# A mixture-of-experts layer: expert rows added by indirect DMA to a sum in DRAM instead of stored and fetched back

## The reference

```
s = sigmoid(x1 @ router_w); two experts per token, from the best of 4 groups
gate = s of the two, divided by their sum
out = sum over the two: gate * ((silu(x1 @ w_gate[e]) * (x1 @ w_up[e])) @ w_down[e])
result = LayerNorm(alpha * x1 + out) * ln2_w + ln2_b
```

## Time and profile before

| | us |
|---|---|
| median of the three runs | 1034.89 |
| span of the profiled execution | 1030.7 |
| TensorE busy in it | 884.6 (86%) |
| VectorE / ScalarE / POOL busy | 667.7 / 455.7 / 139.0 |
| first expert tile starts | 514.1 |
| last matmul ends | 948.8 |

### The profile page before, as it was taken

The page is one execution under the profiler, slowest core; times in us unless marked ns, Lnnn a source line. Parts: engine busy times, 40 slices in busy tenths (PEclk is TensorE's granted clock), DMA queues, the critical chain, the costliest instruction groups (busy, mean ns, idle before and its releaser), DMA issues.

```text
span 1030.7 us, 15075 instructions
## 1 busy us (share of the span) xinstructions
PE 884.6 (86%) x4992; PEld 772.3 (75%) x4992; DVE 667.7 (65%) x981; ACT 455.7 (44%) x594; POOL 139.0 (13%) x168
## 2 busy tenths in 40 slices
PE   6999999999967999995199999999999999998000
PEld 6998887888755888884189898988989898897000
DVE  3441899983265778874837586676898662635695
ACT  3531110102355443313336686767888662645231
POOL 3000011011112112100100001000110100000583
PEclk9999999999996999996599999999999999999555
DMA  7620213314225433314657498695999863595671
GB/s 270 214 83 1 99 54 123 105 73 160 82 85 164 157 108 100 125 41 160 229 224 284 167 405 345 219 392 181 413 407 410 339 224 142 185 324 205 212 259 79
DMA packets 77509, 202.25 MB, mean 196 GB/s; under 512 B 7215, under 2 KB 27009, under 8 KB 77473
## 3 DMA queue, kind: packets, MB, share of 16 engines
q1 hardware_dynamic: 63984, 155.31, 41.8%
q0 software_dynamic: 9888, 33.76, 9.1%
q10 hardware_dynamic: 3600, 12.72, 3.1%
HBM read 167.14 MB, written 34.62 MB: 196 GB/s over the span
## 4 chain that ended last, share of the span: by engine, by line
PE 79%; DVE 9%; issue 7%; DMA 2%; ACT 1%; POOL 1%; DVEq 0%; SPq 0%; POOLq 0%; ACTq 0%
PE banks L1072 17%; PE banks L622 13%; PE banks L611 13%; PE banks L636 13%; PE banks L1069 8%; PE banks L1186 6%; PE banks L595 2%; DVE arena L849 2%; PE banks L1207 2%; PE banks L602 1%; PE banks L1053 1%; DMA arena<-in_x 1%; DVE split_weights L804 1%; PE banks L1121 1%; DVE small L865 1%
## 5 line engine op out<-in xcount | busy, mean ns | idle before, releaser
L804 DVE TENSOR_TENSOR split_weights<-arena,split_weights 128x1024 fp32r<-128x1024 f32 x192 | 223.7, 1218 | 1.0
L654 ACT ACTIVATE split_weights<-arena 128x1024 fp32r<-128x1024 f32 x192 | 190.7, 1052 | 12.2 <-ACT work L691 10.4
L1072 PE MATMUL banks<-split_weights 128*128 128x512 f32 (+2 forms) x960 | 182.5, 351 | 0.0
L1072 PEld LDWEIGHTS banks<-split_weights 128*128 128x128 f32 x960 | 156.2, 191 | 23.9 <-issue 1.4
L622 PE MATMUL banks<-split_weights,split_rows 128*128 128x256 f32 x1152 | 147.5, 284 | 0.0
L622 PEld LDWEIGHTS banks<-split_weights,split_rows 128*128 128x128 f32 x1152 | 142.7, 191 | 1.9
L611 PE MATMUL banks<-split_weights,split_rows 128*128 128x512 f32 x576 | 136.0, 392 | 2.5 <-DVE split_rows L808 2.5
L636 PE MATMUL banks<-split_weights,split_hidden 128*128 128x512 f32 x576 | 137.5, 394 | 0.0
L611 PEld LDWEIGHTS banks<-split_weights,split_rows 128*128 128x128 f32 x576 | 109.1, 190 | 25.6 <-issue 2.9
L636 PEld LDWEIGHTS banks<-split_weights,split_hidden 128*128 128x128 f32 x576 | 106.6, 188 | 21.6
L821 DVE TENSOR_TENSOR work<-work,banks 128x256 f32<-128x256 f32 x48 | 20.2, 421 | 116.0 <-PE banks L622 116.0
(11 more groups left out here) (294 smaller groups left out, 991.2 us busy)
## 6 DMA issues: line engine op xcount, KB each, us to landing
arena<-in_w_gate SPq DMA_DIRECT2D x64, 512.0 KB, 6.2
arena<-in_w_up SPq DMA_DIRECT2D x64, 512.0 KB, 7.2
arena<-in_w_down SPq DMA_DIRECT2D x64, 512.0 KB, 7.9
y_scratch<-work ACTq DMA_DIRECT2D x24, 512.0 KB, 6.6
arena<-in_w_in SPq DMA_DIRECT2D x20, 512.0 KB, 5.5
arena<-in_x SPq DMA_DIRECT2D x16, 512.0 KB, 6.1
arena<-in_w_out SPq DMA_DIRECT2D x8, 512.0 KB, 5.1
x_scratch<-arena SPq DMA_DIRECT2D x8, 512.0 KB, 3.4
```

Source lines behind the costliest of these rows:

```text
L654: act.activation(unit_split(u, 0), unit_slot(u), AF.Copy).then_inc(xw_hi, 1)
L804: dve.tensor_tensor(unit_split(u, 1), unit_slot(u), unit_split(u, 0).bitcast(F32), ALU.subtract).then_inc(xw_lo, 1)
L1072: last = pe.matmul(b[:, 0:width], xT[:, hx, k, j * P:(j + 1) * P], wc[:, hw, k, 0:width], start=(k == 0 and i == 0), stop=(k == KC - 1 and ...
```

## The change

- The mixer stage stores each x1 tile twice: in `x1_dram` and in a new `acc_dram`. Both have 128 rows more at their start, filled with ones, for slots that hold no token; token t is row 128 + t.
- Routing also computes the gate of each slot: three bf16 parts of the gates (divided by alpha) on the one-hots, 16 matmuls, and a sum, `gate_slot`. A second list of rows, `tok_sums`, gives each unused slot a row of its own among the 128. All this comes before the first tile's rows are split.
- ScalarE's copy of a tile's result multiplies it by the slot's gate. Its store is gone. POOL instead adds the 128 rows to `acc_dram` by an indirect DMA with `compute_op=ALU.add`, each add after the one before has landed.
- The last stage waits for all adds, loads 8 tiles of `acc_dram` and normalises them on VectorE (LayerNorm doesn't change if its input is divided by alpha and its epsilon by alpha squared). ScalarE only takes the square root. POOL does nothing in it. The rows `ln2` are loaded at the start of the expert stage.

The core of the diff:

```diff
             def store_x1(ch):
                 sp.wait_ge(x1_ready, ch.c + 1)
-                sp.dma_start(x1_dram[bass.ds(ch.c * P, P), :], x1s).then_inc(x1_out, 16)
+                for rows_out in (x1_dram, acc_dram):
+                    sp.dma_start(rows_out[bass.ds(P + ch.c * P, P), :], x1s).then_inc(x1_out, 16)
...
+            def add_rows(g):
+                pool.wait_ge(y_out, ADDED + 16 * g)
+                pool.tensor_copy(tok_out, tok_sums[:, bass.ds(g, 1)]).then_inc(out_idx_ready, 1)
+                pool.wait_ge(y_sb, PRIMED + g + 1)
+                wait_apart(pool, out_idx_ready, g + 1)
+                pool.indirect_dma_start(out=acc_dram, out_offset=bass.IndirectOffsetOnAxis(ap=tok_out, axis=0), in_=ys,
+                                        in_offset=None, compute_op=ALU.add).then_inc(y_out, 16)
+
+            def body(e, g, last, more):
+                gather(g + 1)
+                add_rows(g)
...
             gather(0, True)
-            total = each_tile(pool, "pool", lambda e, g, last, more: gather(g + 1))
+            for i, src in enumerate((ln2_w[0], ln2_b[0])):
+                pool.dma_start(ln2[:, i, :], src.partition_broadcast(P)).then_inc(y_out, 16)
+            pool.wait_ge(sum_index_ready, 1)
+            total = each_tile(pool, "pool", body)
...
-            wait_apart(pool, y_out, PRIMED + total * 16)
...
+            wait_apart(pool, y_out, ADDED + total * 16)
+            pool.sem_inc(acc_done, 1)
...
+            pe.wait_ge(gate_hot_ready, 1)
+            for i in range(2 * T):
+                last = pe.matmul(bank(3)[:, 0:96], hot_lo[:, i, :], hot_gate[:, i, :], start=(i == 0), stop=(i == 2 * T - 1))
+            last.then_inc(gate_sums_ps, 1)
             transpose_rows(0)
...
                 act.wait_ge(y_ps, g + 1)
-                act.wait_ge(y_out, PRIMED + g * 16)
-                act.activation(ys, psum[:, 2:4, :].rearrange("p a n -> p (a n)"), AF.Copy).then_inc(y_sb, 1)
-                act.wait_ge(y_sb, PRIMED + g + 1)
-                act.dma_start(y_dram[bass.ds(g * P, P), :], ys).then_inc(y_out, 16)
+                act.wait_ge(y_out, ADDED + g * 16)
+                act.activation(ys, psum[:, 2:4, :].rearrange("p a n -> p (a n)"), AF.Copy,
+                               scale=gate_slot[:, bass.ds(g, 1)]).then_inc(y_sb, 1)
...
+            dve.wait_ge(tok_ready, 1)
+            own.link(dve.tensor_scalar(unused, tok[:, :], 0.0, i_tok, ALU.is_equal, ALU.mult))
+            dve.tensor_tensor(tok_sums[:, :], tok[:, :], unused, ALU.add).then_inc(sum_index_ready, 1)
...
+            own.link(dve.tensor_copy(gate_parts[:, 0], gflat2))
+            own.link(dve.tensor_tensor(gate_rest, gflat2, gate_parts[:, 0], ALU.subtract))
+            own.link(dve.tensor_copy(gate_parts[:, 1], gate_rest))
+            own.link(dve.tensor_tensor(gate_parts[:, 2], gate_rest, gate_parts[:, 1], ALU.subtract))
+            for i in range(3):
+                last = dve.tensor_tensor(hot_gate[:, :, i * 32:(i + 1) * 32], hot_tile,
+                                         gate_parts[:, i].unsqueeze(2).to_broadcast([P, 2 * T, 32]), ALU.mult)
+            last.then_inc(gate_hot_ready, 1)
...
-            for u in range(6):
+            for u in range(2):
+                split_lo(0, u)
+            dve.wait_ge(gate_sums_ps, 1)
+            own.link(dve.tensor_copy(gate_sum, bank(3)[:, 0:96]))
+            own.link(dve.tensor_tensor(gate_sum[:, 32:64], gate_sum[:, 32:64], gate_sum[:, 64:96], ALU.add))
+            dve.tensor_tensor(gate_slot, gate_sum[:, 0:32], gate_sum[:, 32:64], ALU.add).then_inc(gates_ready, 1)
+            for u in range(2, 6):
                 split_lo(0, u)
...
+            def finish(t):
+                r = rs_f[:, t:t + 1]
+                dve.wait_ge(fin_std, t + 1)
+                own.link(dve.reciprocal(r, r))
+                dve.scalar_tensor_tensor(final(t), final(t), r, ln2[:, 1, :], ALU.mult, ALU.add).then_inc(out_ready, 1)
+
+            dve.wait_ge(y_out, ADDED)
+            for t in range(T):
+                dve.wait_ge(acc_in[t], 16)
+                for i in range(2):
+                    last = dve.bn_stats(st_c[:, i, :], final(t)[:, i * 512:(i + 1) * 512])
+                wait_apart(dve, dve_own, own.done(last))
+                dve.bn_aggr(mv_f[:, t, :], st_c).then_inc(fin_stats, 1)
+                dve.wait_ge(fin_stats, t + 1)
+                own.link(dve.scalar_tensor_tensor(final(t), final(t), mv_f[:, t, 0:1], ln2[:, 0, :], ALU.subtract, ALU.mult))
                 if t > 0:
+                    finish(t - 1)
+            finish(T - 1)
```

More of the change, by code:

```diff
@@ L51 @@
 TILES_MAX = (2 * SEQ + NE * (P - 1)) // P
-SMALL = 1136
+SMALL = 1160
 UNITS = 12
@@ L68 @@
 PRIMED = 1
+ADDED = 32
 class Chunk:
@@ L321, in hybrid_kernel @@
         packed_sum = at("c", 2)[0:1]
+        gate_rest = at("c", 2 * T)
+        gate_sum = at("c", 96)
+        unused = at("c", 32)
+        gate_parts = at("c", 24).bitcast(BF16).rearrange("p (i n) -> p i n", i=3)
+        hot_gate = at("c", 48 * T * 2).bitcast(BF16).rearrange("p (i n) -> p i n", n=96)
+        used["d"] = 3072
         sil = at("d", DE)
@@ L498, in sp_experts, with final @@
                     load_unit(sp, e, u)
[L500 to L511, removed]
             sp.wait_ge(xw_lo, UNITS * NE)
-            for t in range(SETS):
-                reload_x1(t)
+            sp.wait_ge(acc_done, 1)
             for t in range(T):
-                if t == T - 1:
-                    sp.wait_ge(y_fill, sp.snap(filled))
+                sp.dma_start(final(t), acc_dram[P + t * P:P + (t + 1) * P, :]).then_inc(acc_in[t], 16)
+            for t in range(T):
                 sp.wait_ge(out_ready, t + 1)
[L520 to L530, removed]
+                sp.dma_start(out_tiles[t], final(t)).then_inc(stored, 16)
+            sp.wait_ge(stored, 16 * T)
+        def final(t):
+            return arena[:, t * D:(t + 1) * D]
         def pool_experts(pool, own):
@@ L566, in pool_experts @@
-            for t in range(3):
-                fetch(t)
-            pool.wait_ge(ln2_in, 32)
-            for t in range(T):
-                if t + 3 < T:
-                    fetch(t + 3)
-                pool.wait_ge(scaled_ready, t + 1)
-                pool.tensor_tensor(final(t, 0), final(t, 0), ln2[:, 1, :], ALU.add).then_inc(out_ready, 1)
+            wait_apart(pool, y_out, ADDED + total * 16)
+            pool.sem_inc(acc_done, 1)
         def pe_experts(pe):
@@ L897, in _ @@
                 n += 1
+            sp.wait_ge(made, 3)
+            for rows_out in (x1_dram, acc_dram):
+                sp.dma_start(rows_out[0:P, :].rearrange("p (k n) -> p k n", k=KC),
+                             ones[:, :].unsqueeze(1).to_broadcast([P, KC, P])).then_inc(rows_filled, 16)
             def load_kqv(ch):
@@ L960, in _ @@
             own = Links(pool, sem("pool_own"), "pool_links")
-            for s in (lg_read, x1_out, x1T_ps, lg_ps, y_sb, y_out):
+            for s in (lg_read, x1_out, x1T_ps, lg_ps, y_sb):
                 pool.sem_inc(s, PRIMED)
```

83 lines of the change are left out of this document (24 added, 59 removed).

## The result

The changed kernel takes **1125.14 us** (median of 4 runs, 1121.69 to 1127.24) against 1033.54 us before in the same session: a ratio of 1.089, 95% interval [1.086, 1.092]. It is 92 us slower where I forecast 27, and above my range. The profiled execution took 1121.69 us with a span of 1119.9, so 1.8 us lie outside the span, not the 4.2 I took.

The account below looks back on a forecast made before the run. TensorE paces the expert stage (18.04 us tiles), then a tail without matmuls. Span 1030.7 - 24.6 + 3.9 + 47.6 = 1057.6 us; with 4.2 outside it 1061.8, say 1062 us; range 1021 to 1095.

Parts of the forecast that it names:

- The tail: After the last tile's copy: replacing fetches, scaled additions and POOL's bias additions by reloads and VectorE work saves 24.6 us.
- Before the first tile: Added routing operations on VectorE ahead of the first tile's row split cost 3.9 us, bounds 2.5 and 5.8.
- The moved gather: In each tile POOL's gather of rows two tiles ahead follows the copy wait and add: 14 x 3.4 = 47.6 us.
- S+14.8: Predicted landing of the gather with weights arriving, in us after the tile's gate matmuls start (S); 3.4 us late.
- rival B: TensorE's clock falls in the stalls: 14 x 1.6 = 22 us more, 1084 us; chance 0.13.
- its instruction 0.97 us: In each tile, the time assumed for POOL to issue the add, from S+2.55.
- the constant: Time outside the profiled span, taken as 4.2 us: the median of the runs less the span.
- ScalarE loses the issue of the store: In each tile ScalarE no longer issues the store and gains a scale in its copy; counted as nearly free.
- the 14 tiles with weights arriving: The expert-stage tiles expected to stall, 3.4 us each; the 9 without arriving weights would lose next to nothing.
- Stalls also in the tiles without weights: Expert-stage sign that the forecast was wrong, pointing to rival C or a longer POOL loop than assumed.
- rival C: The add is slow everywhere: gather 11.5 us late in 23 tiles, 265 us more, about 1280 us; chance 0.07.
- the rule I did cite: A DMA that adds issues two reads per piece and halves the rate; used for the add's extra 2.4 us pass.

Follow-up runs that it names:

- The last experiment: The kernel with the gather ahead of the add, plus a final 128x1 POOL copy after VectorE's last result: 1011.5 us, against 1007.24 without it.

## Why the prediction was wrong

**The tail** was 24.6 us by my count and is 31.6: from the copy's end to the end of the span 80.7 before and 49.1 after. From the copy's end to the reloads it takes 1078.20 - 1070.83 = 7.4 us (counted 7.7 + 0.9), to VectorE's start 3.4 more (3.5), then VectorE 35.3 (36.0). The larger part of the 7 us is the end of the program: I carried over 8.0 us, and it is 3.05. The last experiment shows that POOL being last is worth 4 to 5 us.

**Before the first tile**: the first gate matmul starts at 516.70, after a routing chain that began 1.3 us earlier than before. 516.70 - 514.13 + 1.3 = 3.87 us for 3.9.

**The moved gather and the clock behind it** are where the prediction failed, in two steps. The mechanism of the first stands: the wait's place, the order on the queue and the extra pass for the sum gave S+14.8, and in the nine shorter waits 3.9 us were measured for 3.4. The steps that failed are these:
- The clock was left out of the sum (rival B had it, "Against it: here each wait would follow a dense stretch"). It cost 33.3 us.
- The add's issue was priced as "its instruction 0.97 us". It took 1.6 us at best, and 6.9 in six tiles in which VectorE's splits ran without a break. The waits of these six sum to 47.8 us, which at 3.9 each would have been 23.

The accounts close: 1062, and 10 for fifteen waits of 3.9 instead of fourteen of 3.4, 25 for the six long ones, 33 for the clock, less 7 for the tail and 2 for the constant, is 1121, and the profiled execution took 1121.7. By the same sum, as an estimate, the time would have been 1088 without the clock's part, inside my range, and 1096 without the six long waits, still just above it. The kernels with a break bear this out: no long issue is left in them, and they take 1098 and 1101 us.

I had priced each of POOL's instructions by a row in which it was alone or lucky, though the tail of the earlier trace rows held a warning. Of the eight L860 there, the first has no POOL addition beside it and takes 0.16 us; the seven others take 2.1 to 2.3:

```profile
966.87 0.16 DVE L860 SCALAR_TENSOR_TENSOR small<-small 128x1 f32<-128x1 f32 x1
```

The reciprocal that I had compared with is no such pair: six of its eight also ran beside an addition, in 0.16 us. I used the row to price the tail and did not ask whether it holds the other way round. And "ScalarE loses the issue of the store", booked as nearly free, was what took VectorE's break away: 27 us.

The two causes, each with and without the other (time, waits; the break is ScalarE's issue, and the one that VectorE's wait makes agrees within 3.2 us of time and 6 of waits; the 55 us are from the run of 1081 us):

| | eight splits unbroken | with a break |
|---|---|---|
| POOL's wait, no add | 1062 to 1081 us, 55 us | 1026 us, 19 us |
| POOL's wait and the add | 1125 us, 82 us | 1098 us, 61 us |
| gather ahead of the add | 1007 us, 0 us | not run |

**My conditions for a stall were too narrow.** I gave it to the 14 tiles with weights arriving. 15 tiles wait, the last of them with a DMA share of 0.20 over the tile. "Stalls also in the tiles without weights" I had as a sign of rival C, the slow add everywhere; here it was a held issue, and one tile.

**Rival B was no rival but an addition.** The clock fell, and not for 1.6 us a stall but for 33.3 / 15 = 2.2, because down matmuls and transposes stand right behind the wait. I gave it 0.13 as if it excluded the forecast. The long and many waits have it, the short ones don't: with 14 waits of up to 2.0 us slow matmuls are 1.2 us in all, in the kernels with 45 to 82 us of waits 22 to 33. The Trainium skill (TensorE: Matmul & The Clock Gate, "HAM oscillation") describes waits for DMA that send the clock back each time. These runs agree: a granted clock of 0.71 behind the wait shown above, and 7.27 us for down matmuls of 5.73.

Of the rule I did cite, the plain store shows the size here. The Trainium skill (Collectives: The Full Stack, "The bandwidth ceiling") says of ReduceScatter, not of an indirect DMA, that it is slower than AllGather because its addition needs two source reads. The runs agree as far as 6.1 to 6.7 us to the next index copy against 3.5 go, and 41 us over 24 tiles in landing, clock and two fewer held issues together.

The rule that I should have weighed is another. The Trainium skill (SBUF — State Buffer, "Who interferes with whom" and "Summary: rules for kernel authors") says that a VectorE instruction with two inputs in SBUF and a POOL instruction that reads SBUF contend, and that the second one to issue is blocked until the first finishes. The splits have two such inputs, and POOL's copy reads one, so that it waits agrees. But it waited for up to five splits to end, not for one, and in the kernel without adds three of 15 copies didn't wait that long. That page of the Trainium skill infers that a `tensor_tensor` doesn't keep POOL from making a DMA's descriptors; here an add's issue took 6.9 us beside them and the plain store's 6.3. An indirect DMA also reads its row numbers from SBUF, and no run tells whether that read or the descriptors were held. That the shared port is the cause is not shown; the runs show that an issue was never held over 2.61 us where VectorE's row had a break, and in 34 of 74 cases where it had none.

**Open**: what in a break lets POOL in, why a row of splits without a break holds POOL in only about half of the cases, and why the add's instruction takes 1.6 us where a gather takes 1.0. Since the share of held issues differs from trace to trace (six of eight, four of 15), part of a difference between two such kernels may be chance.

## What to carry to other kernels

When an edit puts a wait on an engine's queue, look first at what is queued behind it, and issue that first if it doesn't depend on the wait: here this order alone is worth 118 us. Price a POOL instruction, a DMA issue too, by what VectorE does at that moment, with a range and not one number, and treat an issue that the edit takes off a third engine as a change of rhythm, not as nothing. A stall in front of TensorE has a second price, the slower clock of what follows, so add it to the first instead of holding it as an alternative.

## What the hardware did that I had not expected

- POOL's 128x1 copy took up to 5.2 us and an indirect DMA's issue 6.9 us beside eight two-input VectorE instructions without a break (0.18 and 1.59 at their best), but not every time: 12 of 15 copies in the kernel without adds, 34 of 74 issues. With a break of 0.13 us in the eight no issue took over 2.35 us.
- Less DMA traffic made more of POOL's issues slow, ten instead of six: twelve instead of eight then started in a row of splits without a break.
- The span ended 8.0 and 8.1 us after POOL's last instruction where POOL finished last, and 3.05 us after VectorE's where POOL had long been done.
- An accumulating indirect DMA of 512 KB issued in 1.59 us and landed without traffic after 5.9 (1071.72 to 1077.6).
